# Spreading the gather and scatter of a mixture-of-experts stage over two column blocks each, with other places for two activations

## The reference, cut to what matters

```python
def _swiglu(x, w_gate, w_up, w_down):
    return (jax.nn.silu(x @ w_gate) * (x @ w_up)) @ w_down      # 1024 -> 3584 -> 1024

def _moe_swiglu(x, w_router, b_router, w_gate, w_up, w_down):
    ...                                       # top 2 of 8 experts for each token
    for e in range(N_EXPERTS):
        out = out + combine[..., e:e + 1].astype(x.dtype) * _swiglu(x, w_gate[e], w_up[e], w_down[e])
    return out
```

## Time and profile before

| | |
|---|---|
| median of 3 runs | 2967.05 us (2965.32 to 2967.56) |
| profiled execution, first to last instruction | 2961.7 us |
| mean granted TensorE clock | 0.910 |
| PE busy | 2550.9 us (86%) |
| DVE busy | 2062.3 us (70%) |
| ACT busy | 1557.5 us (53%) |
| weights' queue (q1) | 580.30 MB |

### The profile page before, as it was taken

How to read it: one execution, slowest core, us unless ns; L and a number is a source line. 1 busy time by engine, 2 the same in 40 slices (tenths; PEclk the granted TensorE clock), 3 DMA queues, 4 the chain that set the end, 5 groups by cost and what they waited for, 6 DMA issues and landing times.

```text
span 2961.7 us, 31514 instructions
## 1 busy us (share of the span) xinstructions
PE 2550.9 (86%) x11727; PEld 2001.1 (68%) x11727; DVE 2062.3 (70%) x2214; ACT 1557.5 (53%) x1920; POOL 24.0 (1%) x33
## 2 busy tenths in 40 slices
PE   6977789977967999999999999976777998886898
PEld 2736677856556777777777777765556786655787
DVE  6687786755666888787878888875665554575454
ACT  1222434442156778787777777764534544544443
POOL 0000000000100000000000000000000000000000
PEclk8997999986978999999999999998877999977899
DMA  7450367732335898898989899984112454303352
GB/s 252 160 164 29 106 214 263 270 120 71 100 114 200 323 332 324 300 361 291 362 302 353 330 333 329 335 295 136 44 43 100 157 185 156 109 15 114 104 188 93
DMA packets 274306, 598.03 MB, mean 202 GB/s; under 512 B 28705, under 2 KB 35167, under 8 KB 272993
## 3 DMA queue, kind: packets, MB, share of 16 engines
q1 hardware_dynamic: 252144, 580.30, 55.2%
q10 hardware_dynamic: 22002, 15.66, 2.0%
HBM read 594.86 MB, written 1.06 MB: 201 GB/s over the span
## 4 chain that ended last, share of the span: by engine, by line
PE 61%; DVE 24%; ACT 10%; issue 2%; ACTq 2%; DMA 1%; DVEq 0%; POOL 0%; POOLq 0%; PEldq 0%
PE PS L205 58%; DVE WL L167 8%; ACT WH L197 3%; ACT AR L197 2%; PE PS L213 2%; DVE MW L167 2%; DVE AR L167 2%; ACTq L146 2%; DVE WF L167 1%; DVE MOD L167 1%; ACT MW L197 1%; ACT L197 1%; DVE HF L167 1%; ACT WF L197 1%; DVE HTR L167 1%
## 5 line engine op out<-in xcount | busy, mean ns | idle before, releaser
L167 DVE TENSOR_TENSOR WL<-RG,WH 128x1024 fp32r<-128x1024 f32 (+1 forms) x558 | 919.4, 1648 | 447.4 <-ACT WH L197 422.8
L197 ACT ACTIVATE WH<-RG 128x1024 fp32r<-128x1024 f32 x782 | 827.3, 1058 | 597.4 <-PE PS L205 527.2
L205 PE MATMUL PS<-WH,HTR 128*128 128x512 f32 (+3 forms) x2920 | 926.0, 393 | 66.8 <-DVE HTR L167 23.4
L205 PEld LDWEIGHTS PS<-WH,HTR 128*128 128x128 f32 x2920 | 558.0, 194 | 201.0 <-DVE WL L167 39.8
L205 PE MATMUL PS<-WL,HTR 128*128 128x512 f32 (+3 forms) x1460 | 568.9, 390 | 0.0
L205 PE MATMUL PS<-WH,ATR 128*128 128x512 f32 x1624 | 523.6, 396 | 16.4 <-DVE WL L167 9.1
L205 PEld LDWEIGHTS PS<-WH,ATR 128*128 128x128 f32 x1624 | 310.3, 191 | 84.7 <-DVE WL L167 18.3
L205 PE MATMUL PS<-MW,HTR 128*128 128x512 f32 x1332 | 331.1, 398 | 18.2 <-DVE MW L167 18.2
L205 PE MATMUL PS<-WL,ATR 128*128 128x512 f32 x812 | 320.4, 395 | 0.0
L205 PEld LDWEIGHTS PS<-WL,HTR 128*128 128x128 f32 x1460 | 283.2, 194 | 52.4
L167 DVE TENSOR_TENSOR MW<-RG,MW 128x2048 fp32r<-128x2048 f32 x112 | 256.7, 2292 | 63.3 <-ACT MW L197 52.6
(11 more groups left out here) (224 smaller groups left out, 2057.5 us busy)
## 6 DMA issues: line engine op xcount, KB each, us to landing
RG<-in_moe_w_gate SPq DMA_DIRECT2D x112, 1024.0 KB, 5.4
RG<-in_moe_w_up SPq DMA_DIRECT2D x112, 1024.0 KB, 5.8
RG<-in_moe_w_down SPq DMA_DIRECT2D x112, 1024.0 KB, 6.0
RG<-in_w_ff SPq DMA_DIRECT2D x64, 1024.0 KB, 5.2
RG<-in_mod_w SPq DMA_DIRECT2D x48, 1024.0 KB, 5.2
RG<-in_w_in SPq DMA_DIRECT2D x36, 1024.0 KB, 5.2
RG<-in_w_out SPq DMA_DIRECT2D x16, 1024.0 KB, 5.1
RG<-in_ffn_w_gate SPq DMA_DIRECT2D x14, 1024.0 KB, 5.2
```

The lines of the kernel that those rows point to most:

```text
L167: return self.did(lambda: self.e.tensor_tensor(o, a, b, op))
L197: return self.did(lambda: self.e.activation(o, a, f, bias=bias, scale=scale))
L205: return self.did(lambda: self.e.matmul(o, l, r, start=start, stop=stop))
```

## The change

TensorE: half g = 0 of the gather stays at n = 3, half g = 1 moves to n = 4, put_back moves from n = 4 to n = 5; half t = 0 of the scatter stays at n = 1, t = 1 moves to n = 2.

ScalarE: the eight scale-and-bias instructions are cut into four pairs, put behind the copies of gate A and of gate B of the next iteration, at n = 3 and n = 4; HE's high part moves to n = 5; the transposes' eviction moves from the end of the iteration to the next one, behind the copy of up A; silu moves behind the copy of down A.

VectorE: HE's low part moves to n = 5, the additions of t = 1 to n = 2, and the low part of the transposes behind the low part of the next up A. No instruction of the experts' stage is added or dropped, and the order in which weights are loaded is the same.

```diff
@@ pe_moe
-                if n == 3 and e + 1 < NE:
-                    gather(e + 1)
-                if n == 4 and e + 1 < NE:
+                if n in (3, 4) and e + 1 < NE:
+                    gather(e + 1, n - 3)
+                if n == 5 and e + 1 < NE:
                     put_back(e + 1)
-                if n == 1 and e:
-                    scatter(e - 1)
+                if n in (1, 2) and e:
+                    scatter(e - 1, n - 1)
                 if j:
                     down(j - 1)
...
@@ v_moe
+            def low(j):
+                u = j % 2
+                v.wait_ge(s_a, j, "at")
+                v.tt(EAT[1][:, u], four(4 + 2 * u), EAT[0][:, u].bitcast(F32), SUB).then_inc(s_v, "at")
...
-                P.los(v, 8 if j else 4)
+                P.los(v, 2)
+                if j:
+                    low(j - 1)
+                P.los(v, 6 if j else 2)
...
-                if n == 1 and e:
-                    scatter(e - 1)
+                if n in (1, 2) and e:
+                    scatter(e - 1, n - 1)
                 P.los(v, 4)
...
-                if n == 3 and e + 1 < NE:
+                if n == 5 and e + 1 < NE:
                     gather(e + 1)
-                v.wait_ge(s_a, j, "at")
-                v.tt(EAT[1][:, u], four(4 + 2 * u), EAT[0][:, u].bitcast(F32), SUB).then_inc(s_v, "at")
+            low(len(todo) - 1)
@@ a_moe
-                P.his(a, 4)
+                more = e + 1 < NE
+                P.his(a, 2)
+                if j:
+                    evacuate(j - 1)
+                P.his(a, 4 if j else 2)
                 a.wait_ge(P.used, P.of["moe_gate", e, n][-1].i + 1)
                 if j >= 2:
                     a.wait_ge(s_v, j - 2, "ac")
                 a.act(ESG[:, u], PS[:, 4 + 2 * u, :], ACT.Silu).then_inc(s_a, "sg")
                 if j:
-                    P.his(a, 4)
-                if n == 3 and e + 1 < NE:
-                    gather(e + 1)
-                if n == 4 and e + 1 < NE:
+                    P.his(a, 2)
+                P.his(a, 2)
+                if n in (3, 4) and more:
+                    modulate(e + 1, n - 3, (0, 1))
+                P.his(a, 2)
+                if n in (3, 4) and more:
+                    modulate(e + 1, n - 3, (2, 3))
+                if n == 5 and more:
+                    for g in range(2):
+                        gathered(e + 1, g)
                     put_back(e + 1)
-                P.his(a, 4)
...
-                if j >= 2:
-                    a.wait_ge(P.used, P.of[("moe_down", *todo[j - 2])][-1].i + 1)
-                a.wait_ge(s_pe, j, "at")
-                a.act(EAT[0][:, u], four(4 + 2 * u), ACT.Copy).then_inc(s_a, "at")
+            evacuate(len(todo) - 1)
```

More of the change, by code:

```diff
@@ L1943, in pe_moe, with gather @@
         def pe_moe(pe, P, s_pe, s_v, s_a):
-            def gather(e):
+            def gather(e, g):
                 u = e % 2
                 pe.wait_ge(s_v, e, "pp")
[L1947 to L1958, removed]
+                if e:
+                    pe.wait_ge(s_a, e - 1, f"gm{g}")
+                    if e > 1:
+                        pe.wait_ge(s_v, e - 2, f"acc1{g}")
+                    if g == 0:
+                        pe.wait_ge(s_a, e - 1, "pt")
+                for k in range(4):
+                    for t in range(2):
+                        x = pe.mm(PS[:, 2 + g, k * 128:(k + 1) * 128], X[:, t, (g * 4 + k) * 128:(g * 4 + k + 1) * 128],
+                                  PP[:, u, t], t == 0, t == 1)
+                x.then_inc(s_pe, f"ga{g}")
             def put_back(e):
@@ L1974, in up, with scatter @@
                     x.then_inc(P.used)
-            def scatter(e):
+            def scatter(e, t):
                 u = e % 2
                 pe.wait_ge(s_a, e, "pt")
[L1979 to L1988, removed]
+                for h in range(2):
+                    c = slice(h * 512, (h + 1) * 512)
+                    pe.wait_ge(s_v, e, f"de{h}")
+                    if t:
+                        pe.wait_ge(s_v, e, f"acc0{h}")
+                    elif e:
+                        pe.wait_ge(s_v, e - 1, f"acc1{h}")
+                    pe.mm(PS[:, 2 + h, :], PT[:, u, tok(t)], DE[0][:, c], True, False)
+                    pe.mm(PS[:, 2 + h, :], PT[:, u, tok(t)], DE[1][:, c], False, True).then_inc(s_pe, f"sc{t}{h}")
             def down(j):
@@ L2003, in down @@
                     x.then_inc(P.used)
-            gather(0)
+            for g in range(2):
+                gather(0, g)
             put_back(0)
@@ L2030, in pe_moe @@
             down(len(todo) - 1)
-            scatter(NE - 1)
+            for t in range(2):
+                scatter(NE - 1, t)
         def v_moe(v, P, s_pe, s_v, s_a, part, beside=nothing):
@@ L2049, in gather, with scatter @@
                          SUB).then_inc(s_v, f"he{g}")
[L2051 to L2057, removed]
+            def scatter(e, t):
+                for h in range(2):
+                    c = slice(h * 512, (h + 1) * 512)
+                    v.wait_ge(s_pe, e, f"sc{t}{h}")
+                    v.stt(ACC[:, t, c], PS[:, 2 + h, :], CW[:, e, t:t + 1], ACC[:, t, c], MUL, ADD).then_inc(
+                        s_v, f"acc{t}{h}")
             def results(e):
@@ L2082, in v_moe, with modulate, gathered, evacuate @@
                     choose(e + 1)
-                if n == 3 and e + 1 < NE:
+                if n == 5 and e + 1 < NE:
                     gather(e + 1)
-                v.wait_ge(s_a, j, "at")
-                v.tt(EAT[1][:, u], four(4 + 2 * u), EAT[0][:, u].bitcast(F32), SUB).then_inc(s_v, "at")
+            low(len(todo) - 1)
             results(NE - 1)
-            scatter(NE - 1)
+            for t in range(2):
+                scatter(NE - 1, t)
         def a_moe(a, P, s_pe, s_v, s_a, beside=nothing):
[L2091 to L2100, removed]
-                    x.then_inc(s_a, f"gm{g}")
[L2102 to L2105, removed]
+            def modulate(e, g, ks):
+                a.wait_ge(s_pe, e, f"ga{g}")
+                if e:
+                    a.wait_ge(s_v, e - 1, f"he{g}")
+                for k in ks:
+                    c = 48 + 32 + g * 4 + k
+                    x = a.act(GM[:, g, k, :], PS[:, 2 + g, k * 128:(k + 1) * 128], ACT.Identity, scale=MC[:, c:c + 1],
+                              bias=MC[:, c - 8:c - 7])
+                if 3 in ks:
+                    x.then_inc(s_a, f"gm{g}")
+            def gathered(e, g):
+                if e >= 2:
+                    a.wait_ge(P.used, P.of["moe_up", e - 2, 6][-1].i + 1)
+                a.act(HE[0][:, e % 2, g * 4:g * 4 + 4, :], GM[:, g], ACT.Copy).then_inc(s_a, f"he{g}")
+            def evacuate(j):
+                if j >= 2:
+                    a.wait_ge(P.used, P.of[("moe_down", *todo[j - 2])][-1].i + 1)
+                a.wait_ge(s_pe, j, "at")
+                a.act(EAT[0][:, j % 2], four(4 + 2 * (j % 2)), ACT.Copy).then_inc(s_a, "at")
             def put_back(e):
@@ L2118, in results @@
                     a.act(DE[0][:, h * 512:(h + 1) * 512], PS[:, h, :], ACT.Copy).then_inc(s_a, f"de{h}")
-            gather(0)
+            for g in range(2):
+                modulate(0, g, range(4))
+            for g in range(2):
+                gathered(0, g)
             put_back(0)
```

## The result

| | before | changed |
|---|---|---|
| median of the timed runs | 2967.31 us | 2898.91 us |
| ratio, 95% interval | | 0.9769 [0.9757, 0.978] |
| profiled span | 2961.7 | 2900.2 |
| start of the first gate matmul to start of the last scatter ("the stage") | 1073.1 | 1007.3 |

The kernel is 68.4 us faster by the medians, 65 to 72 by the interval; 61 were forecast. The stage tells it more sharply: it is 65.8 us shorter, and came out at 1007.5 in a second profile of the changed kernel. Around it nothing is changed, yet the first gate matmul starts anywhere between 910.8 and 917.9 us in the profiles of this study (910.95 before, 917.17 after). When the changed kernel was measured again, one execution ran at a granted clock of 0.291 and took 8333 us; it is left out.

What follows compares the result with a forecast made beforehand. TensorE's work, with holes left by the weights' preparation, was taken as the bound. Per expert 124.6 + 1.25 + 0.3 (0.55 at four of seven) = 126.15 against 134.86; 7 × 8.7 = 61 saved, 2967 to 2906 us; range 2896 to 2933.

Steps and rivals of the forecast that it cites:

- Scatter in two iterations: At the scatter, PE's wait for the first addition and its slow running go: 2.3 + about 1.5 us per expert.
- Gather in two iterations: Holes behind the gather and at the following up A go: 2.35 + 1.4 us per expert, with some slow running.
- The ScalarE schedule: At the gather, scale-and-bias pairs fit between copies: the first costs nothing, the second delays up A's copy from 0.9 to 1.55.
- The tightest place: n = 1, behind the results: up A 0.15, up B 0.4 late, PE 0.5 late; with n = 3, 1.15 to 1.25 us per expert.
- a plain iteration is TensorE's own and stays at 17.0; this part gives nothing by itself: Moving eviction and silu behind copies leaves plain iterations at 17.0 us; it gives only reserve for the rest.
- what is still lost: Holes left per expert: 1.25 + 0.3 us (0.55 at four of seven), on 124.6 us of TensorE's work.
- A: VectorE's backlog replaces the waits, with gate A at n = 2 coming 2 us late: 27 us, so 2933; chance 0.16.
- B: Weight transfers bound stretches without holes, plain iterations 17.7 us at 355 GB/s or so: 22 us, 2928; chance 0.08.
- C: Slower: the weight slots' cycle breaks from landings of 9 us on, 73 us lost against 61 saved, 2979; chance 0.04.
- D: The spread of gather and scatter does nothing, each half waiting for its bank as before: 2967; chance 0.02.

Runs made afterwards that it cites:

- e2: Kernel before with only the scatter split, half t = 0 at n = 1 and t = 1 at n = 2; 2938.68 us, ratio 0.9908.
- e3: Kernel before with only the gather split, scale and bias in pairs, put_back and the gathered tile's parts at n = 5; 2948.41 us, ratio 0.9931.
- e10: Kernel before with the eviction behind the next up A's copy and silu behind down A's copy; 2947.64 us, ratio 0.9931.
- e4: Changed kernel with the expert's results moved from the end of n = 0 to behind up B's copy and low part at n = 1; 2893.03 us.
- e7: Kernel before with ScalarE's eviction of the transposes done twice; 2991.76 us, ratio 1.0082.
- e1: Kernel before with only the eviction moved behind the next up A's copy, its low part to match on VectorE; 2960.46 us, ratio 0.9976.
- e11: Changed kernel with both halves of the scatter at n = 1 again; 2925.13 us, ratio 0.9857.
- e9: e4 with choose two experts ahead at n = 6 instead of one ahead at n = 2, and the work beside at n = 4; 2892.02 us.

## Why the prediction came out right, and where it didn't

**The sign and the size: right; the place in part.** 61 us were forecast, the stage gave 65.8, the medians 68.4. Seven scatters and seven gathers carry most of it: e2 alone gives 23.1 and e3 alone 19.2. The activations' places, forecast at nothing, give 15.9 (e10). Together that is 58.2; the remaining 7.6 exist only in company. They fit above all the growth of n = 6 in e3, 1.3 by the medians, of which the changed kernel keeps 0.3.

**Scatter in two iterations: right.** 2.3 + 1.5 = 3.8 us per expert forecast; undone in the changed kernel it costs 25.6 / 7 = 3.7.

**Gather in two iterations: right.** The forecast 3.75 us with some slow running were 4.4 at n = 3 and n = 4 of e3; taken by itself the gather's split loses part of that again at n = 6, and much less of it beside the other edits. The ScalarE schedule holds; the changed kernel's rows at its n = 3, ScalarE:

```profile
1103.15 1.06 ACT L197 ACTIVATE MW<-RG 128x1024 fp32r<-128x1024 f32 x1 [0.44 <-PE PS L205]
1104.51 1.06 ACT L197 ACTIVATE MW<-RG 128x1024 fp32r<-128x1024 f32 x1 [0.30 <-PE PS L205]
1106.29 0.95 ACT L197 ACTIVATE AR<-PS,SMALL 128x128 f32<-128x128 f32 x2 [0.73 <-PE PS L205]
1107.67 1.07 ACT L197 ACTIVATE WH<-RG 128x1024 fp32r<-128x1024 f32 x1 [0.42 <-PE PS L205]
```

The pair lies where ScalarE would wait for TensorE anyway: 0.73 before it, and still 0.42 behind it.

**The tightest place: VectorE's schedule was right to a tenth, but for the results.** The schedule had the results end at 2.2, up A's low part at 5.7, up B's at 8.9 and gate A's at 18.9 us of n = 1. VectorE's rows, with gate A of n = 1 at 1055.75:

```profile
1056.83 1.49 DVE L167 TENSOR_TENSOR DER<-PS,DER 128x512 fp32r<-128x512 f32 x2
1059.10 2.29 DVE L167 TENSOR_TENSOR WL<-RG,WH 128x2048 fp32r<-128x2048 f32 x1 [0.78 <-ACT WH L197]
...
1062.30 2.29 DVE L167 TENSOR_TENSOR MW<-RG,MW 128x2048 fp32r<-128x2048 f32 x1
...
1072.42 2.29 DVE L167 TENSOR_TENSOR MW<-RG,MW 128x2048 fp32r<-128x2048 f32 x1
```

They end at 2.6, 5.6, 8.8 and 19.0. TensorE, however, asked 0.17 us earlier for up B than the rows of before had it, so the same times were more late than forecast. e4 shows that this lag at n = 1 is the results' doing.

**Wrong: "a plain iteration is TensorE's own and stays at 17.0; this part gives nothing by itself".** It wasn't: a loop through the eviction held it at 17.0 (e7), and down A's copy behind silu at 16.9 (e1, e10). The two places gave 15.9 us of the stage by themselves. The sign was in the rows I cited. ScalarE waited for the transposes in 42 iterations, and its next copy fed the second matmul group after them; I read this as idle time of an engine with room. I also took a period without an idle row for TensorE's own, where a pair of matmuls lasted 0.77 instead of 0.62; such pairs, of 0.74 to 0.77 us, stand in some thirty places of the stage.

**Mis-sized, and hidden by that: what is still lost.** TensorE's work per expert is 7 × 16.79 for the plain part; with 1.81 for each half gather (18.59 at n = 4), 0.26 for put_back and 0.91 for each half scatter it is 123.2, not 124.6. So 2.7 us per expert remain in holes, not 1.55. They lie at n = 1 (0.8), n = 2 (0.6), n = 3 (0.6) and n = 6 (0.9 by the median, 1.1 to 1.2 in the four experts with `beside`); I had 0.55, 0.5, 0.1 and 0.3 (0.55 in those four). I followed VectorE's lag through n = 2 and wrote 0.2 us of reserve for the next gate A, at the start of n = 3, where there was none. The two errors, 1.4 too much work and 1.2 too little loss, nearly cancel within an expert: that the forecast of 126.15 came within 0.2 us of 125.95 is luck in part.

**The rivals.** A (backlog in place of the waits) is the right mechanism at a third of its price, (2.7 − 1.55) × 7 = 8 us over the forecast: nothing was late by 2 us. (Its sum 7 × 15.9 + 8 is 119.3, not 119.6; nothing hangs on that.) B did not come: ScalarE waited 1.1 us for data in the stage. In the stage's last, plain iterations of 16.79 us the weights' 6.29 MB are a demand of 375 GB/s. The window over four of them:

```profile
core 0: us, PE busy (x) PEld busy (x) DVE busy (x) ACT busy (x) POOL busy (x), PEclk, DMA share, GB/s
...
1847.80:1914.90 67.10, 67.10 (x305) 55.63 (x304) 61.70 (x34) 54.77 (x55) 0.00 (x0) 1.00 0.98 359
```

The queue brought 359 GB/s there, and TensorE had no hole; the difference over 67.1 us is 1.1 MB, about one slot of the ring. So these four iterations don't show that 375 could be held for long. The 358 GB/s that the Trainium skill, "DMA: Bandwidth & Descriptors", section "Where 436 GB/s comes from", gives for one core did not bind here: the kernel before drew 379 over 51 us, and over six experts the changed kernel drew no more than 352. By that figure a plain iteration would have been 17.6 us; it was 16.79. C did not come either, with landings at 6.2 us. D is refuted by n = 1.

## What to carry to other kernels

An iteration without an idle row isn't proof that its busiest engine bounds it. Follow the chain once around; where an idle engine waits for the busy one and then feeds it, double one instruction in that wait (here 0.6 us more of ScalarE gave 0.6 us per iteration). Work whose result is needed late should stand behind the copy that feeds the next matmul, and work with two halves on one buffer should be split over two iterations, so long as what its first consumer needs isn't pushed past its due time. Side work goes where the second engine has room, not where it is merely not asked for yet.

## What the runs showed of the hardware

- The weights' loads held 352 GB/s over 755.7 us, with the DMA share at 0.97, and the median landing of down's loads was 6.2 us, against 6.0 at 329 GB/s in the kernel before.
- Holes of up to 0.7 us before gate A left the granted clock at 1.00 over six experts; behind a hole of 2.94 us four matmuls took 2.09 instead of 1.07 (e11). The slow running isn't the same each time: behind the seven holes of 2.89 to 2.94 us in e11 it was 2.02 to 2.09 six times and 1.60 once, and behind six of 2.22 to 2.37 us in the kernel before it was 1.59 three times and 2.02 to 2.09 three times.
- The start of the first gate matmul wandered by 7 us between profiles, in code ahead of it that is the same in all of them. A change of 4 us in the stage (e1, e9 against e4) is seen in the iterations and hardly in the median.
